# The values panel of a gated linear recurrence: eight feature-major products and four PE transposes, in place of token-major products of 128 columns

## The reference

```python
u = rms_norm(h, norm1_g[l]) * (1 + sc1) + sh1
z = u @ w_in[l]
zq, zf, zi, zg, zca, zcb, zga, zgb = jnp.split(z, IN_SPLITS, axis=-1)
f = lb + (1.0 - lb) * jax.nn.sigmoid(zf.astype(jnp.float32))
o = hgrn2_chunkwise(heads(zq), heads(1.0 - f), heads(zi), heads(jnp.log(f)))
o = rms_norm(o, hg_norm_g[l].reshape(HG_HEADS, HG_DV))
y_a = (o * jax.nn.silu(zg)) @ w_a[l]
```

## Time and profile before

| | |
|---|---|
| time, median of 3 runs | 4413.63 us (4413.58 to 4416.94) |
| profiled execution, its own time | 4412.64 us |
| its span | 4410.9 us |
| mean granted PE clock | 0.93 |
| PE, DVE, ACT, POOL busy | 91%, 55%, 30%, 29% |
| stage of the heads | 93.7 to 520 us of the span |

### The profile page before, as it was taken

One profiled execution on the slowest core, in us unless ns is written; L12 is line 12 of the kernel. 1 busy time (PEld: TensorE's weight loads), 2 busy tenths in 40 slices (PEclk: granted clock), 3 DMA queues, 4 the chain that ended last, 5 costly groups with the idle time before them and its releaser, 6 DMA issues.

```text
span 4410.9 us, 52602 instructions
## 1 busy us (share of the span) xinstructions
PE 3996.0 (91%) x17356; PEld 3073.1 (70%) x17356; DVE 2429.9 (55%) x4466; ACT 1341.6 (30%) x1887; POOL 1281.5 (29%) x524
## 2 busy tenths in 40 slices
PE   7988799889999999979999997978699989778998
PEld 6877455667888887867888885833488866336886
DVE  2566666751787878617777773044363312664442
ACT  2444211223344343411111112254222224442221
POOL 1211000233433434334444442400144433003442
PEclk7999899999999999989999998988899998669999
DMA  4212333222454636476566651210122222002222
GB/s 137 82 48 81 109 114 114 77 72 86 122 162 143 206 99 199 136 224 197 179 196 179 199 151 57 96 52 25 39 91 95 94 74 92 25 17 76 96 96 77
DMA packets 266636, 486.52 MB, mean 110 GB/s; under 512 B 16721, under 2 KB 148177, under 8 KB 266097
## 3 DMA queue, kind: packets, MB, share of 16 engines
q1 hardware_dynamic: 86544, 316.71, 22.4%
q10 hardware_dynamic: 179972, 168.17, 12.5%
HBM read 415.48 MB, written 84.02 MB: 113 GB/s over the span
## 4 chain that ended last, share of the span: by engine, by line
PE 47%; issue 38%; POOL 9%; DVE 4%; ACT 2%; POOLq 0%; ACTq 0%; DVEq 0%
PE ps L335 13%; PE ps L336 13%; PE ps L337 13%; POOL ring_r L1651 9%; PE ps L642 3%; PE ps L626 2%; DVE st L1195 1%; PE ps L373 1%; PE ps L635 1%; ACT arena L1086 1%; DVE sq L1216 1%; DVE arena L1533 0%; DVE arena L1598 0%; DVE st L1204 0%; DVE st L1199 0%
## 5 line engine op out<-in xcount | busy, mean ns | idle before, releaser
L1651 POOL TENSOR_TENSOR ring_r<-ring,high_w 128x1024 fp32r<-128x1024 f32 x520 | 1281.3, 2465 | 3091.1 <-ACT high_w L727 2519.0
L335 PE MATMUL ps<-uT_r,high_w 128*128 128x512 f32 x2496 | 1001.3, 401 | 140.2 <-DVE sq_r L1221 69.8
L337 PE MATMUL ps<-uT_r,ring_r 128*128 128x512 f32 x2496 | 981.1, 393 | 0.0
L336 PE MATMUL ps<-sq_r,high_w 128*128 128x512 f32 x2048 | 803.8, 392 | 0.0
L727 ACT ACTIVATE high_w<-ring 128x1024 fp32r<-128x1024 f32 x392 | 413.6, 1057 | 1104.8 <-PE ps L337 929.7
L336 PE MATMUL ps<-part,high_w 128*128 128x512 f32 x1856 | 737.3, 397 | 0.0
L335 PEld LDWEIGHTS ps<-uT_r,high_w 128*128 128x128 f32 x2496 | 475.0, 190 | 249.9 <-issue 90.2
L335 PE MATMUL ps<-part,high_w 128*128 128x512 f32 x1536 | 613.7, 400 | 2.0 <-POOL ring_r L1651 2.0
L337 PE MATMUL ps<-part,ring_r 128*128 128x512 f32 x1536 | 607.8, 396 | 0.0
L337 PEld LDWEIGHTS ps<-uT_r,ring_r 128*128 128x128 f32 x2496 | 474.0, 190 | 102.7
L336 PEld LDWEIGHTS ps<-sq_r,high_w 128*128 128x128 f32 x2048 | 388.9, 190 | 78.4
(11 more groups left out here) (248 smaller groups left out, 4369.8 us busy)
## 6 DMA issues: line engine op xcount, KB each, us to landing
ring<-panels SPq DMA_DIRECT2D x600, 512.0 KB, 3.5
adram<-act_out ACTq DMA_DIRECT2D x128, 256.0 KB, 3.9
gdram<-arena ACTq DMA_DIRECT2D x16, 2048.0 KB, 11.7
arena<-gdram ACTq DMA_DIRECT2D x128, 256.0 KB, 5.9
arena<-adram ACTq DMA_DIRECT2D x128, 256.0 KB, 2.7
strips_dram<-btab ACTq DMA_DIRECT2D x4, 3584.0 KB
arena<-strips_dram ACTq DMA_DIRECT2D x32, 448.0 KB, 3.3
hT<-xT ACTq DMA_DIRECT2D x1, 2048.0 KB, 14.2
```

The costliest lines, as they stand in the source:

```text
L335: t_.matmul(out, wh, xh, start=(k == 0), stop=False)
L336: t_.matmul(out, wh, xl, start=False, stop=False)
L337: last = t_.matmul(out, wl, xh, start=False, stop=(k == KT - 1))
L1651: g_.tensor_tensor(ring_r[:, j], ring[:, j], high_w[:, j], ALU.subtract).then_inc(lo_ready, 1)
```

## The change

G2 becomes an ordinary `panel`. ACT copies its feature-major result from bank 2 into a new buffer `vt_head` (where it filled `vb` before), and PE turns it back with four transposes of 128x128 into the same bank (`head_turn`, placed behind G0 of the next head). ACT then copies the bank into `vb` and only then frees it. Two semaphores are new, `vt_copied` (ACT to PE) and `vt_turned` (PE to ACT). For head 7 the turn stands ahead of `head_off(7)`.

```diff
+        vt_head = view(18432, T)
...
             def head_gemm(q8, j0, n, ready=None):
-                if n == 2:
-                    panel_tok(q8, j0 + 2, (uT_r, ulo))
-                else:
-                    panel(q8, j0 + n, (uT_r, ulo), ready=ready)
+                panel(q8, j0 + n, (uT_r, ulo), ready=ready)
+
+            def head_turn(h):
+
+                pe.wait_ge(vt_copied, h * 1 + 1)
+                for tt in range(TT):
+                    last = t_.transpose(ps[:, 2, tt * P:(tt + 1) * P], vt_head[:, tt * P:(tt + 1) * P], ident)
+                last.then_inc(vt_turned, 1)
 
             def head_step(h, hh, q8n, jn, nxt=True, before=True):
 
                 if nxt:
                     head_gemm(q8n, jn, 0)
+                head_turn(h)
+                if nxt:
                     head_gemm(q8n, jn, 1)
                 head_off(h)
...
+            head_turn(7)
             head_off(7)
...
                 taken(q8, j0 + 2)
-                s_.activation(vb[:, hh], ps[:, 2, :].rearrange("p (a b) -> p a b", a=TT), ACT.Copy).then_inc(bank_free[2], 1)
+                s_.activation(vt_head, ps[:, 2, :], ACT.Copy).then_inc(vt_copied, 1)
                 taken(q8, j0 + 3)
                 s_.activation(gb[:, hh, :], ps[:, 3, :], ACT.Silu).then_inc(bank_free[3], 1)
+                act.wait_ge(vt_turned, h * 1 + 1)
+                s_.activation(vb[:, hh], ps[:, 2, :].rearrange("p (a b) -> p a b", a=TT), ACT.Copy).then_inc(bank_free[2], 1)
                 if ahead >= 1:
                     for j in (2, 3):
                         high(q8, j0 + 4 + j)
```

More of the change, by code:

```diff
@@ L260, in build @@
         lvl_done, lvl_evac, v_free = sem("lvl_done"), sem("lvl_evac"), sem("v_free")
+        vt_copied, vt_turned = sem("vt_copied"), sem("vt_turned")
         o_copied, osq_ready, og_ready = sem("o_copied"), sem("osq_ready"), sem("og_ready")
@@ L339, in panel @@
                         last = t_.matmul(out, ring[:, j % RING, k, :], x[:, k, 0:n], start=(k == 0), stop=(k == KT - 1))
[L340 to L352, removed]
                 last.then_inc(gemm_done, 1)
```

## The result

| | before | changed |
|---|---|---|
| time, median | 4414.57 us (4413.58 to 4416.94, 4 runs) | 4465.77 us (4463.36 to 4471.87, 4 runs) |
| profiled execution, time and span | 4412.64, 4410.9 us | 4463.36, 4461.5 us |
| ratio, 95% interval | | 1.0117 [1.01, 1.0135] |

A forecast was written before the change was run, and what follows sets the result against it. Each head was taken as a chain across PE and DVE, with ACT's logarithm feeding the scans. 8.4 us in each of heads 1 to 6, +50.4, less 4.0 in head 0, made +46.4: 4460 us, range 4433 to 4467.

The forecast's parts named there:

- G2's saving is worth nothing in heads 1 to 6: PE, heads 1 to 6: the 5.1 to 5.3 us saved only lengthen the 5.73 us idle time behind G2.
- The late logarithm as the cause: ACT, heads 1 to 6: waiting for the turn delays the logarithm, so DVE's scans could begin 7.8 us later.
- The blocked scan and the half clock: DVE's scans blocked while POOL computes, 6 x 1.6 = 10 us; PE at half clock after 5.4 us idle. Chance of both 0.55.
- the term from `head_off` to `head_mean`: PE's stretch, mostly at half clock: 5.3 us taken, against 3.26 at full and 5.98 at half clock.
- levels 2 to 4 (0.4): PE's levels 2 to 4 behind the longer idle time: 0.4 us added per head, between 0 and 0.8.
- Head 0: G2's saving counts twice here: levels 2 to 4 start 4.0 us earlier, between 3 and 6.6.
- behind head 6: Head 7: the turn is covered by PE's 12.00 us wait for `koff`: 0; without that cover 0.9 us.
- The free scan at full clock (4432): Rival, heads 1 to 6: late logarithm without scan block or clock loss, `head_mean` 4.2 us late, +19 us; chance 0.17.
- That the wait is hidden: Rival: DVE's idle time ahead of `head_mean` takes up the delay, only head 0 gains 4 to 6 us, 4409; chance 0.05.
- the limit that the prediction gives for it: DVE's 4.16 us idle ahead of `head_mean`: hidden only if the logarithm is at most 4.2 us late.
- That saved PE time counts as such: Rival: each of 8 heads gains the narrow matmuls' 5.1 us less 0.36, 38 us, 4375; chance of faster 0.06.

The follow-up runs named there:

- e7: The changed kernel with ACT's copy into `vb` behind the logarithm, PE's G3 ahead of levels 2 to 4 and G1 behind level 1: 4369.50 us, ratio 0.9892.
- e8: The kernel before, narrow G2 kept, with PE's G3 ahead of levels 2 to 4 and G1 behind level 1: 4391.48 us, ratio 0.9942.
- e1: The changed kernel with ACT's wait for the turn and copy into `vb` moved behind the logarithm and exponentials of `koff`: 4413.04 us, ratio 0.9991.
- e4: The kernel before plus one ACT wait, for PE's G0 of the next head, ahead of the high parts and logarithm: 4466.36 us, ratio 1.0113.
- e2: The changed kernel with two high parts ahead of ACT's wait for the turn and two equal-sized unused copies in their place: 4450.07 us, ratio 1.0076.
- e3: The changed kernel with 20 unused PE products of 512 columns between G1 and `head_off`: 4449.07 us, ratio 1.0074.
- e10: The changed kernel with the high parts of G2 and G3 ahead of ACT's wait for the turn, nothing in their place: 4429.22 us, ratio 1.0025.
- e9: e7 with G3's high part held until DVE has taken the last level, and G1 ahead of `head_off` in head 0: 4348.43 us, ratio 0.9844.

## Why the prediction was right

The mechanism held step by step. The time, 4465.77 us, is 5.8 over the forecast of 4460 and only 1.2 under the upper end of its range; the terms below that were too small or too favourable all err the same way.

**G2's saving is worth nothing in heads 1 to 6: right.** Idle time behind G2 went from 5.73 to 10.82 us. e7 and e8 show the counterpart: its worth of 4.7 us per head once PE is the bound.

**The late logarithm as the cause: right,** by e1 from the one side and e4 from the other. Its steps held within 0.15 us: transposes at p+7.9 (forecast p+7.87), ACT at p+8.55 (p+8.51), scans' end at p+16.2 (p+16.05), `head_off` at p+19.46 (p+19.38).

**The blocked scan and the half clock: right in kind.** e2 took the first away: 16 us by the medians, 13 by the spans. By the trace 6 x 1.55 = 9 come from the scans' own time, 4 from a shorter slow stretch (5.0 us from `head_off` to `head_mean` on average, not 5.66) and 3 from head 0 (its score product at 156.61); what lies behind head 6 took 3 us more in that execution. Of head 0's 3 us, 1.2 are an earlier silu (117.99, not 119.19), which e2's edit doesn't reach. e3 took the second away: `head_mean` at p+22.83 instead of p+25.12, 2.3 us in each of six heads, 14 in all (p to p 54.82, 13 in six heads). Mis-sized was the term from `head_off` to `head_mean`: I took 5.3 us, it was 5.12 to 6.14, 5.66 on average, so that `head_mean` came 8.4 us late instead of 8.0; with 0.33 us on levels 2 to 4 (0.4) that makes 8.7 us per head instead of 8.4. That is 1.9 us of the 4.3 that the profiled execution's +50.7 has over the forecast's +46.4.

**Head 0: right in sign, too large.** It gave back 2.8 us, not 4.0. Its silu came at 119.19, not 117.8. The stage's first panel began at 93.94 (93.75 before), but PE had the full clock only from 99.84 on, where it had it from 96.97 on in the kernel before. Windows of the changed kernel, and of the kernel before:

```profile
93.94:99.83 5.89, 5.89 (x14) 4.63 (x15) 4.06 (x7) 3.71 (x7) 2.10 (x1) 0.50 0.00 0
```
```profile
93.75:96.96 3.21, 3.21 (x8) 2.53 (x9) 3.21 (x6) 3.21 (x7) 0.00 (x0) 0.50 0.00 0
```

Nothing in the change stands ahead of that point, and the other traces show that it is chance from one execution to the next: e2, whose code is the changed kernel's up to there, had the full clock from 97.15 on, and e8, whose code is the kernel before's, only from 99.85 on. The 1.1 us behind head 6 were forecast as 0; e2's 3 us at the same place show that executions differ by more than that.

**The rivals.** The free scan at full clock (4432) failed by the two rows above: 3.06 us for the scans and a granted clock of 0.50. That the wait is hidden failed as forecast, but the limit that the prediction gives for it, 4.2 us from DVE's idle time ahead of `head_mean`, was read from the wrong wait: that idle time ends with PE's column sum, and what a late logarithm can use up is the time that `koff` is ready ahead of `head_off`, 3.7 us (p+9.78 to p+13.49). e10 bears this out: its scans start 6.0 us later than before in head 2 (p+11.19, not p+5.23) and `head_mean` is 2.5 us late, so 3.5 us were hidden. The delay of 7.8 us was over both. That saved PE time counts as such failed: busy PE time fell by 15 us and the time rose by 51. That another order of the work could bring this rival about, as the prediction left open, is what e7 and e8 show.

## What to carry to other kernels

Where an engine works through a fixed list, an added wait costs what stands behind it in the list, not what it waits for: look for the first instruction behind it that another engine's chain hangs on, and put the waiting instruction behind that. Before shortening a product, read whether idle time follows it; if it does, first move other work of the same engine into that place, and only then does the shorter product pay. And a piece of work that becomes late can meet new company: here it met POOL's, and then PE's lowered clock, and these two made some 23 of the 51 us (9 by e2's scans, 14 by e3).

## What the runs showed of the hardware that I had not expected

- Useless products made the kernel faster: 20 of them in a wait (e3) saved 12 to 17 us, because the 3.3 us of small products behind it then ran at 2.4 GHz instead of taking up to 6.1 us.
- PE lost the full clock already behind 3.8 us of idle time in e2, and around the 3.3 us of e7. Behind 1.7 to 1.8 us it kept it in e9 and e10, but not always: in e8, in one of six heads with the same wait (head 3, p at 257.10), it was granted 1.2 GHz from 267.10 to 270.51, just behind 1.83 us of idle time. That head alone took 44.7 us from p to p, the other five 42.9 to 43.1. So in these traces an idle time of 1.8 us is no safe one. PE in that head, and the window (columns as in the earlier trace rows):

```profile
266.98 0.65 PE L406 MATMUL ps<-arena 128*128 128x128 f32 x2 [1.83 <-DVE arena L1303]
```
```profile
267.10:270.51 3.41, 3.41 (x13) 3.05 (x14) 2.49 (x8) 2.17 (x4) 0.00 (x0) 0.50 0.25 102
```

- A DVE `tensor_scalar` of 0.41 us from the work buffer into itself took 2.35 us beside POOL (e7), while the reciprocal took 3.35 us whether POOL worked inside it (e9) or not. That alone doesn't show that a reciprocal can't be blocked: in none of these traces does one start while POOL is at work, and POOL's remainders that began inside it took their usual 2.35 to 2.41 us. What did start beside POOL and took its usual time is `copy_predicated` with its data from PSUM, 0.72 to 0.77 us in either case. So not all kinds of DVE work are blocked.
